# Compression of keys and the first attention in one block, the attention opening with the last token tile's uncompressed branches

## The reference

```python
def compress(k_raw, pe, w1, b1, w2):          # 31 blocks of 32 tokens, stride 16, two groups
    blocks = k_raw[:, idx] + pe
    hid = silu(flat(blocks) @ w1 + b1)        # 2048 -> 256
    return hid @ w2                           # 256 -> 64

kc = rope(rms_norm(compress(kc_raw, ...), nsa_kc_gain), cmp_pos)
vc = compress(vc_raw, ...)
o_cmp = softmax(q . kc, blocks ended by t) . vc
o_sel = softmax(q . ks, chosen blocks, <= t) . vs     # 8 blocks, 16 may be chosen: all
o_win = softmax(q . kw, window of 512, <= t) . vw
g = sigmoid(gate_logits)
o_nsa = (g0 * o_cmp + g1 * o_sel + g2 * o_win) * silu(z_n)
o_dsa = softmax(qd . kd, the top-k keys by an index score) . vd * silu(z_d)
out = x + concat(o_nsa, o_dsa) @ w_out
```

## Time and profile before

| what | value |
|---|---|
| runs | 3018.84, 3019.22, 3013.61 us; median 3018.84 |
| profiled execution | 3014.08 us, span 3012.3 us |
| TensorE busy | 2911.4 us, 97% of the span |
| VectorE busy | 2329.1 us, 77% |
| ScalarE busy | 1125.3 us, 37% |
| GpSimd busy | 131.0 us, 4% |
| mean granted TensorE clock | 0.987 |

### The profile page before, as it was taken

How to read it: one execution, slowest core, us unless ns; L and a number is a source line. 1 busy time by engine, 2 the same in 40 slices (tenths; PEclk the granted TensorE clock), 3 DMA queues, 4 the chain that set the end, 5 groups by cost and what they waited for, 6 DMA issues and landing times. The chain is left out here.

```text
span 3012.3 us, 43721 instructions
## 1 busy us (share of the span) xinstructions
PE 2911.4 (97%) x16784; PEld 2575.3 (85%) x16784; DVE 2329.1 (77%) x4062; ACT 1125.3 (37%) x1850; POOL 131.0 (4%) x99
## 2 busy tenths in 40 slices
PE   8999989999999999999999999999999999999998
PEld 7786558899999886788999998899999877779997
DVE  6666757798988776657888888798888855578886
ACT  4335545333323423334332234433233423254443
POOL 2331420000000000000000000000000000000000
PEclk9999999999999999999999999999999999999999
DMA  6423032233433241222333333133333230223332
GB/s 198 120 77 103 22 116 88 92 120 119 126 114 110 78 137 36 69 70 68 115 119 119 102 116 92 63 119 119 113 101 120 73 102 10 68 84 99 99 99 91
DMA packets 317538, 292.78 MB, mean 97 GB/s; under 512 B 12562, under 2 KB 269844, under 8 KB 315796
## 3 DMA queue, kind: packets, MB, share of 16 engines
q1 hardware_dynamic: 317332, 289.98, 31.5%
HBM read 284.18 MB, written 2.10 MB: 95 GB/s over the span
## 5 line engine op out<-in xcount | busy, mean ns | idle before, releaser
L2560 PE MATMUL PS<-hid_f,w_hi 128*128 128x512 f32 (+1 forms) x2464 | 563.8, 345 | 6.2 <-DVE hid_f L2776 6.2
L2560 PEld LDWEIGHTS PS<-hid_f,w_hi 128*128 128x128 f32 x2464 | 389.2, 188 | 65.2 <-DVE hid_f L2776 7.6
L2549 PE MATMUL PS<-x_hi_f,w_hi 128*128 128x384 f32 (+1 forms) x1216 | 390.8, 321 | 0.0
L2549 PE MATMUL PS<-x_lo_f,w_hi 128*128 128x384 f32 (+1 forms) x1216 | 390.7, 321 | 0.0
L2549 PE MATMUL PS<-x_hi_f,w_lo 128*128 128x384 f32 (+1 forms) x1216 | 390.6, 321 | 0.0
L2560 PE MATMUL PS<-hid_f,w_lo 128*128 128x512 f32 x1232 | 338.9, 344 | 0.0
L2641 ACT ACTIVATE w_hi<-w_raw 128x512 fp32r<-128x512 f32 (+1 forms) x420 | 244.8, 604 | 203.1 <-DMA w_raw<-in_w_ffn_dram 138.1
L2144 DVE SCALAR_TENSOR_TENSOR ada_product<-ada_w,ada_s 128x1024 f32<-128x1024 f32 x228 | 278.4, 1221 | 28.1 <-DMA ada_w<-in_w_ada_dram 24.2
L2549 PE MATMUL PS<-t_hi_f,w_hi 128*128 128x384 f32 (+1 forms) x912 | 293.3, 322 | 0.0
L2549 PE MATMUL PS<-t_hi_f,w_lo 128*128 128x384 f32 (+1 forms) x912 | 293.0, 321 | 0.0
L2549 PE MATMUL PS<-t_lo_f,w_hi 128*128 128x384 f32 (+1 forms) x912 | 293.0, 321 | 0.0
(11 more groups left out here) (394 smaller groups left out, 5303.7 us busy)
## 6 DMA issues: line engine op xcount, KB each, us to landing
w_raw<-in_w_ffn_dram SPq DMA_DIRECT2D x256, 512.0 KB, 4.6
ada_w<-in_w_ada_dram SPq DMA_DIRECT2D x120, 512.0 KB, 3.5
w_raw<-in_w_in_dram SPq DMA_DIRECT2D x46, 512.0 KB, 5.2
w_raw<-in_w_out_dram SPq DMA_DIRECT2D x24, 512.0 KB, 6.6
ada_s<-in_conditions_dram SPq DMA_DIRECT2D x7, 1024.0 KB, 5.1
ada_room<-in_w_ada_dram SPq DMA_DIRECT2D x14, 512.0 KB, 3.8
q_plain<-in_w_ada_dram SPq DMA_DIRECT2D x10, 512.0 KB, 4.4
w_raw<-in_w_ffn_dram SPq DMA_DIRECT2D x16, 256.0 KB, 2.8
```

Of the source, the lines that this page charges most:

```text
L2549: last = nc.tensor.matmul(bank_of(kind), wt[:, k, :], xt[:, k0 + k, :], start=(k == 0 and one == 0), stop=(k == 3 and one == 2))
L2560: last = nc.tensor.matmul(ps[:, a:e], wt[:, f, :], hid[:, f, v, a:e], start=(start and f == 0 and one == 0), stop=(end and f == n - 1 and ...
```

## The change

`compress` becomes a class whose methods `attend_first` calls, so that there is one block and no barrier between the two. In that block:

- Units of token tile 3 come as sel, win, cmp; the other tiles keep their order. `FirstUnit` is told its place (`nth`), since the first branch of a tile opens its output and the third closes it with `silu(z)`.
- TensorE runs 12 filler matmuls in place of 20, `hidden(0)`, then `hidden(1)` with the eight rows of unit 0 at its odd steps, then the eight rows of unit 1 with a filler behind each and the values' two small steps at j = 1 and 4; then `turn(0)`. The key transposes come at item 1 of unit 0, a wait for the finished compressed keys and the one row of unit 2 at item 5.
- VectorE no longer does eight rounds ahead of the norm; they move behind the first score, to unit 0. The norm stands among the maxima of unit 1. The ada tile moves too.
- ScalarE takes the conditions' silu and the keys' root behind all four `silu_z`.
- On SyncE's queue the conditions move behind the small loads; w_out's loads wait for `hidden(0)`, the ada loads for `hidden(1)`, since the values' w1 lies in the ada buffers now (four tiles of room instead of three).

```diff
-    order = [(t, b) for t in (3, 2, 0, 1) for b in (("cmp", "sel", "win", "dsa") if t == 0 else ("cmp", "sel", "win"))]
+    branches = {t: ("sel", "win", "cmp") if t == QT - 1 else ("cmp", "sel", "win") for t in range(QT)}
+    units = [FirstUnit(t, b, n) for t in (3, 2, 0, 1) for n, b in enumerate(branches[t] + (("dsa",) if t == 0 else ()))]
-    rounds_at = [1, 4, 5, 1, 5, 5, 0, 0, 0, 0, 0, 2]
+    rounds_at = [8, 6, 0, 1, 5, 5, 1, 1, 1, 1, 1, 1]
...
         @block.sync
+            cmp.load(sp)
+            for dst, name in zip(tabs, ("neg_eye", "cmp_neg")):
+                sp.dma_start(dst[:], dram[name]).then_inc(tabs_in, 16)
+            cmp.load_more(sp)
+            share.ada.load_small(sp)
+            share.load_conditions(sp)
+            sp.wait_ge(cmp.hid_done, 1)
             ring = Ring(c)
             ring.load_ahead(sp, c.step, cols_step(ring, dram["w_out"], ALL_TILES))
+            sp.wait_ge(cmp.hid_done, 2)
...
         @block.tensor
-            pe.wait_ge(rounded, 1)
-            row(0, 0)
+            def beside_values(j):
+                if j == 4:
+                    cmp.turn_hidden(pe, 0)
+                if j == 9:
+                    cmp.output(pe, 0)
+                if j % 2:
+                    if j == 1:
+                        pe.wait_ge(rounded, 1)
+                    row(0, j // 2)
+
+            c.keep_warm(12, 6)
+            cmp.hidden(pe, 0)
+            cmp.hidden(pe, 1, beside_values)
             for j in range(units[1].row_items):
                 row(1, j)
-                nc.tensor.matmul(c.PS[:, 4 + j % 2, 0:P], c.ident[:], c.ident[:], start=True, stop=True)
-                if j == 2:
-                    turn(0)
+                nc.tensor.matmul(c.PS[:, 2 + j % 2, 0:P], c.ident[:], c.ident[:], start=True, stop=True)
+                if j == 1:
+                    cmp.turn_hidden(pe, 1)
+                if j == 4:
+                    cmp.output(pe, 1)
+            pe.wait_ge(cmp.made, 1)
+            turn(0)
...
-                if i == 0:
-                    for j in range(m * 4, m * 4 + 4):
-                        row(2, j)
+                if (i, m) == (0, 1):
+                    pe.wait_ge(moved, 2)
+                    cmp.turn_keys(pe)
+                if (i, m) == (0, 5):
+                    cmp.wait_made(pe)
+                    row(2, 0)
...
         @block.scalar
             copy_q(0)
+            cmp.open_gates(act)
+            cmp.silu(act, 0)
+            cmp.move(act, 0)
+            for t in range(2):
+                cmp.silu_z(act, t)
+            cmp.squares(act)
+            cmp.silu(act, 1)
+            cmp.move(act, 1)
+            for t in range(2, QT):
+                cmp.silu_z(act, t)
+            share.silu(act)
+            cmp.root(act)
             move(0)
...
         @block.vector
+            cmp.gather(dve, 0)
+            cmp.gather(dve, 1)
             ch.link(nc.vector.memset(Mx[:], 0.0))
-            for i in range(2):
-                maxes(i)
             for n in range(early):
                 pick(n)
+            maxes(0)
+            cmp.sum_squares(dve)
+            maxes(1, range(4))
+            cmp.values(dve)
+            cmp.norm_keys(dve, ch)
+            maxes(1, range(4, units[1].row_items))
...
                 if i == 0:
+                    for m in mine:
+                        select(m)
+                    mine = []
+                    cmp.keys_lo(dve)
                     maxes(2)
...
+ADA_FIRST = [0, 1, 0, 0, 1, 1, 0, 0, 0, 0, 1, 1, 1, 2, 2, 1]
...
-            rest = AdaShare(c.ada, s_c, bufs, room[:, 2], [0, 1, 1, 0, 1, 1, 0, 0, 0, 0, 0, 1, 1, 1, 2, 1], (), share)
```

More of the change, by code:

```diff
@@ L1107, in project_first @@
     ring.ahead = False
[L1110 to L1130, removed]
-        room = c.hT.rearrange("p k n -> p (k n)")
[L1132 to L1161, removed]
-                    if i == 0:
[L1163 to L1215, removed]
-                for i in range(2):
[L1218 to L1242, removed]
-            @block.gpsimd
-            def _(pool):
-                nc.gpsimd.memset(G[:, :, :, :, N_CMP:CMP_PAD], 0.0).then_inc(zeroed, 1)
-                pool.wait_ge(zeroed, 1)
-                nc.gpsimd.memset(KLc[HD:HD + 4].bitcast(F32), 1.0).then_inc(zeroed, 1)
-                pool.wait_ge(zeroed, 2)
-                nc.gpsimd.memset(Vc[:], 1.0).then_inc(zeroed, 1)
-            @block.vector
[L1253 to L1261, removed]
-                    dve.wait_ge(stacked, i + 1)
-                    dve.wait_ge(shifted, i + 1)
-                    for g in range(GROUPS):
-                        for part in range(2):
-                            src = S[:, i, g, part * CMP_STRIDE:part * CMP_STRIDE + N_CMP * CMP_STRIDE].rearrange(
-                                "p (c j two) -> p j c two", c=N_CMP, two=2)[:, :, :, 0]
-                            js = slice(part * 8, part * 8 + 8)
-                            last = nc.vector.tensor_tensor(G[:, i, js, g, 0:N_CMP], src,
-                                                           pe_t[:, i, js, None].to_broadcast([P, 8, N_CMP]), ALU.add)
-                    last.then_inc(gathered, 1)
-                gather(0)
-                gather(1)
-                topk.rounds(ch, 8)
-                for i in range(len(share.tiles) - 1):
-                    share.vector(dve, ch, i)
-                dve.wait_ge(squared, 1)
-                nc.vector.reduce_sum(ss[:], sq[:], AX_X).then_inc(summed, 1)
-                dve.wait_ge(rooted, 1)
-                dve.wait_ge(w2_in, 96)
-                ch.link(nc.vector.reciprocal(inv[:], rt[:]))
-                ch.link(nc.vector.tensor_tensor(kraw[:], kraw[:], inv[:, :, None].to_broadcast([CMP_PAD, GROUPS, HD]), ALU.mult))
-                ch.link(nc.vector.tensor_tensor(kraw[:], kraw[:], gain[:, None, :].to_broadcast([CMP_PAD, GROUPS, HD]), ALU.mult))
-                nc.vector.tensor_tensor(A[:], kraw[:], cos[:, None, :].to_broadcast([CMP_PAD, GROUPS, HD]), ALU.mult)
-                for a in range(2):
-                    lo, hi = a * 32, a * 32 + 32
-                    last = nc.vector.tensor_tensor(B[:, :, lo:hi], kraw[:, :, 32 - lo:64 - lo],
-                                                   sin[:, None, lo:hi].to_broadcast([CMP_PAD, GROUPS, 32]), ALU.mult)
-                ch.link(last)
-                for a in range(2):
-                    last = nc.vector.tensor_tensor(R2[:, :, a, :], A[:], B[:], ALU.add)
-                last.then_inc(normed, 1)
-                share.vector(dve, ch, len(share.tiles) - 1)
-                dve.wait_ge(tabs_in, 16 * len(tabs))
-                dve.wait_ge(zeroed, 3)
-                dve.wait_ge(kmoved, 1)
-                ch.link(nc.vector.tensor_tensor(KLc[0:HD].rearrange("p g c -> p (g c)"), c.PS[0:HD, 4, 0:GROUPS * CMP_PAD],
-                                                KKc[0:HD].rearrange("p g c -> p (g c)").bitcast(F32), ALU.subtract))
-                dve.wait_ge(out_done, 2)
-                ch.link(nc.vector.tensor_scalar(Vc[0:CMP_PAD, :, 0:HD], c.PS[0:CMP_PAD, 5, 0:GROUPS * HD].rearrange("p (g d) -> p g d", g=GROUPS),
-                                                valid[:], None, ALU.mult))
@@ L1319, in __init__, with attend_first @@
         self.row_items = HEADS // self.per_row
-def attend_first(c, sb, rows, O, Q, KK, KL, KKc, KLc, Vx, Vc, topk, tri, tabs, gates, dram, share):
+def attend_first(c, sb, cmp, rows, O, Q, KK, KL, KKc, KLc, Vx, Vc, topk, tri, tabs, gates, dram, share):
     nc = c.nc
-    order = [(t, b) for t in (3, 2, 0, 1) for b in (("cmp", "sel", "win", "dsa") if t == 0 else ("cmp", "sel", "win"))]
-    units = [FirstUnit(t, b) for t, b in order + [(t, "dsa") for t in range(1, QT)]]
+    branches = {t: ("sel", "win", "cmp") if t == QT - 1 else ("cmp", "sel", "win") for t in range(QT)}
+    units = [FirstUnit(t, b, n) for t in (3, 2, 0, 1) for n, b in enumerate(branches[t] + (("dsa",) if t == 0 else ()))]
+    units += [FirstUnit(t, "dsa", 3) for t in range(1, QT)]
+    tabs_in = c.tally("cmp_tabs_in").sem
     n_units = len(units)
-    rounds_at = [1, 4, 5, 1, 5, 5, 0, 0, 0, 0, 0, 2]
+    rounds_at = [8, 6, 0, 1, 5, 5, 1, 1, 1, 1, 1, 1]
     sc_at = topk.at
@@ L1348, in attend_first @@
     chosen_mask = sb("chosen", [P, 9 * P], F32R)
-    co, tmp = sb("co", [P, 2, HEADS]), sb("o_tmp", [P, 2, HEADS, HD])
+    co, tmp = sb("co", [P, 2, HEADS]), cmp.T.rearrange("p i (h d) -> p i h d", h=HEADS)
     first, row_first = [0], [0]
@@ L1529, in _ @@
                     keep(i, 0)
+                if n == 1:
+                    cmp.keys_hi(act)
                 for t in turns_at.get((i, n - first[i]), ()):
@@ L1557, in add @@
                 u = units[i]
-                if u.branch == "cmp":
+                if u.opens:
                     return
@@ L1563, in add @@
                 new = tmp[:, i % 2].rearrange("p h d -> p (h d)")
+                if u.branch == "dsa" or u.closes:
+                    pool.wait_ge(cmp.gated, 1 + QT)
```

(27 more changed lines are left out.)

169 lines of the change are left out of this document (167 added, 2 removed).

## The result

The changed kernel takes 3031.71 us, median of five runs (3031.01 to 3034.98), beside 3018.64 us for the one before: a ratio of 1.0050, 95% interval 1.0035 to 1.0064. I had forecast 3018.8 and no change; it is 13 us slower and outside the range. The profiled execution after is the slowest of its five (span 3033.2 us) and the one before was among the fastest, so the 20.9 us between the two spans overstate the difference; their places are what I read from them.

A forecast was written before the change was run, and what follows sets the result against it. TensorE, busy 97% of the span, was taken to bound the kernel. Terms 4.4 - 3.0 + 1.0 = +2.4 us, added to the executions' mean of 3016.4, gave 3018.8 us (no change told), range 3008 to 3030.

The forecast's parts named there:

- The opening: Up to the first score: TensorE waits for VectorE's maxima behind norm and root; first score 266.3 against 263.36, +3.0 us.
- First unit: (3,sel) where (3,cmp) was: 13.8 us plus 1.5 for half clock, 15.3; VectorE's eight rounds just hidden.
- second: Second unit, (3,win): the same items meet in the new order, 17.3 us against 17.15; 14.77 if the stall goes.
- Third unit: (3,cmp): eight narrower rows ahead, VectorE about 1.75 us late, some half clock left: 9.6 us.
- Fourth to sixth: Units from (2,cmp): fifth loses idle 1.1 us and 1.6 us of half clock; 27.5 instead of 30.46, -3.0 us.
- The relief that I argued from: Fifth unit: the rounds and ada tile that made VectorE late are behind it, so idle and half clock go.
- Units 7 to 16: One added top-k round each in five units, mostly held by VectorE's 32.8 us idle: +1.0 us, bounds 0 and 7.5.
- rival A: Clock stays 0.50 through the first unit after the opening's stall: 3024.8 us; chance 0.30 together with a full VectorE.
- B: Whole stage faster: root's chain covered, VectorE relieved, second unit 14.77; -8.4 us, some 3010.4; chance 0.22.
- C: Opening: four maxima stand behind norm_keys on VectorE, the +3.0; alone 3021.8 us; chance 0.48 shared with no change.
- the six terms: Opening, first, second and third units (together +4.4 us), fourth to sixth (-3.0), seventh to sixteenth (+1.0): +2.4 us.

The follow-up runs named there:

- the last but one run: Changed kernel with VectorE lists altered, keys' norm last, conditions' silu earlier, fillers behind first turn and in third unit, top-k rounds split around keys_lo: 3011.35 us, 0.9979.
- the lists and the norm: Changed kernel with top-k rounds and ada tiles redistributed on VectorE, keys' norm behind all second-unit maxima, conditions' silu earlier on ScalarE: 3021.43 us, 1.0002.

## Why the prediction was wrong

- *The opening* was right: first score 266.96 (forecast 266.3), TensorE idle for 4.74 us until VectorE's maxima, behind the norm, behind ScalarE's root, which ended at 258.43 + 0.29 = 258.72 (forecast 258.2). The 1.4 us that the drain of the Trainium skill ("ScalarE: Activation LUTs", section "What ACT_TABLE_LOAD costs") would have put ahead of the root is not there: 257.14 + 1.28 is 258.42, and the root starts at 258.43.
- *First unit* 15.81 (15.3), *second* 18.61 (17.3): near, the second 1.3 us short.
- *Third unit* 12.69 (9.6). I had VectorE 1.75 us late; TensorE's wait was 2.67 and the clock fell behind it, which I had priced as "some half clock".
- *Fourth to sixth, the step that failed*: 35.8 us where I wrote 27.5 and booked a gain of 3.0. The relief that I argued from was there in the fifth alone, and smaller. The earlier trace rows cuts the sixth unit at its second item; its first score before was at 322.93, so that the two took 13.42 and 11.65 us, not 14.87 and 10.20 (the sum is the same):

```profile
322.93 0.39 PE L1433 MATMUL PS<-Q,KK 128*128 128x512 f32 x1
309.51:322.93 13.42, 12.31 (x51) 6.71 (x49) 9.31 (x21) 6.78 (x12) 6.42 (x5) 0.87 0.13 41
322.93:334.58 11.65, 10.73 (x47) 6.05 (x46) 11.01 (x23) 6.30 (x11) 3.31 (x3) 1.00 0.13 45
```

  The sixth was the same after, 11.63 us; the fifth took 11.86 once the clock held, a gain of 1.6. But I let the clock recover at the unit's edge, as it had in the kernel before (1.00 from the first score on, and low for only 3.4 us, 311.8 to 315.2, at the fifth unit's gap of 1.11); here TensorE was busy 23.58 of 23.70 us without getting it back. The three other runs that keep the gap of 2.67 us (the norm last, the stall filled, the rounds moved early) show the same 23.9 us behind it. Filling the gap, with nothing else changed, gives 7 us back.
- *Units 7 to 16*: +5.1 us in the profile, where I took 1.0 from bounds of 0 and 7.5. Partly the ada tile and round in the eleventh, ahead of maxima that the twelfth unit waits for (1.8 us), partly the 10.2 us of half clock instead of 3.4 (3.2 us in the eighth and ninth units), which the change is not shown to have caused. That VectorE has 32.8 us idle there says nothing: an addition hurts if it stands ahead of the maxima that the next unit waits for.
- *The prediction's rival A* had the right mechanism, but I tied it to the opening's stall and the first unit, and by my own test there (a clock under 0.75; it was 0.81) it did not hold. That its price of 6 us lies near the 10 that fillers return is luck: in the first unit they return 2.1 (15.81 to 13.75). The gap that decided was one that I had in the sum as a delay of 1.75 us and not as a cause. Its *B* came near in time (3010.4) only for a kernel with the orders mended and fillers (the last but one run, 3011.35), whose second unit took 16.96 us and not its 14.77; its *C*, that the opening is held by the norm's place on VectorE, held.

In the profiles the six terms miss by 0.7, 0.5, 1.3, 3.1, 8.3 and 4.1 us in this order, 18.0 of the 18.5 us between my +2.4 and the 20.9 of the spans.

What stays open is when the clock falls and for how long. Gaps of 0.46 and 0.36 us did nothing in one run and 1.03 us cost 20 us of half clock in another; but the changed kernel's gap of 2.44 us in the twelfth unit did nothing, and in the five other runs that have it the clock fell behind it in three. In all four runs with fillers in the third unit the clock fell in the fourth or fifth unit, with no gap over 0.36 us in it or in the unit before, for 3.4 to 10.2 us, so gaps aren't all that brings it down there. And each kernel has one profile, while its executions differ: with the lists and the norm, four took 3014.2 to 3016.6 us at a mean granted clock of 0.986 or 0.987 and six 3021.3 to 3022.8 at 0.984 or 0.985. The runs show that filling this gap takes most of the half clock behind it away; they show no limit.

## What to carry to other kernels

Price a gap on TensorE by more than its own length: here the half clock behind one gap lasted from 3.4 to 23.9 us, longest ahead of two compressed units, though no run put other work behind the same gap to show that these are the reason. Fillers in the gap are the cheapest test of it. When a list moves work on an engine that feeds another, look at what is queued behind the added piece, not at the engine's free time in the stage. And fill all gaps of an opening: here, with one of two left, the clock fell there.

## What the runs showed of the hardware

Some of VectorE's operations slow down while GpSimd runs. With the norm moved behind the maxima, two of its products fell beside GpSimd's spread and took 1.09 and 1.01 us, not the 0.28 of the one ahead of them, which both take in the changed kernel too (the run with lists and norm):

```profile
259.70 0.28 DVE L1275 TENSOR_TENSOR cmp_kraw<-cmp_kraw,cmp_inv 32x128 f32<-32x128 f32 x1
260.02 1.09 DVE L1276 TENSOR_TENSOR cmp_kraw<-cmp_kraw,cmp_gain 32x128 f32<-32x128 f32 x1
261.15 1.01 DVE L1277 TENSOR_TENSOR cmp_a<-cmp_kraw,cmp_cos 32x128 f32<-32x128 f32 x1
...
259.94 2.08 POOL L1591 TENSOR_TENSOR qr<-row_max_t,neg_eye 4x512 fp32r<-4x512 f32 x2 [33.03 <-ACT row_max_t L1526]
```

An ada product of 1.22 us took 2.10 beside such a spread (start 379.37, run with the tile moved), and the spread 3.01 instead of 2.03. Row maxima, which read PSUM, kept their 0.68 beside the spread of the kernel before. The Trainium skill, "SBUF — State Buffer", section "Who interferes with whom", says that a VectorE instruction with two SBUF inputs contends with a GpSimd instruction that reads SBUF; the rows agree.
